# A two-layer encoder trunk on one core: arrays laid out for the kernel by the host, the opening reordered, and warm-up matmuls on TensorE

## What is computed

```
x += 0.5 * SwiGLU(RMSNorm(x))        # D_FF = 2816
x += Mixer(RMSNorm(x))               # layer 0: pooling || Hyena long convolution; layer 1: 2-D neighbourhood attention
x += 0.5 * SwiGLU(RMSNorm(x))
swiglu(x) = (silu(x @ wg) * (x @ wu)) @ wd
rmsnorm(x) = x * rsqrt(mean(x*x) + 1e-6) * g
```

## Time and profile before

| | |
|---|---|
| time, median of 3 runs | 1912.54 us (1911.01 to 1912.54) |
| span of the profiled execution, first to last instruction | 1909.3 us |
| around the span, to the median | 3.2 us |
| PE busy (matmul) | 1887.2 us, 99% |
| DVE / ACT / POOL busy | 921.8 / 647.1 / 79.7 us |
| DMA | 180.34 MB, mean 94 GB/s |
| chain that ended last | PE 98%, DVE 1% |

### The profile page before, as it was taken

How to read it: one execution, slowest core, us unless ns; L and a number is a source line. 1 busy time by engine, 2 the same in 40 slices (tenths; PEclk the granted TensorE clock), 3 DMA queues, 4 the chain that set the end, 5 groups by cost and what they waited for, 6 DMA issues and landing times.

```text
span 1909.3 us, 23383 instructions
## 1 busy us (share of the span) xinstructions
PE 1887.2 (99%) x8579; PEld 1537.3 (81%) x8579; DVE 921.8 (48%) x1166; ACT 647.1 (34%) x859; POOL 79.7 (4%) x63
## 2 busy tenths in 40 slices
PE   6999999999999999999999999999999999999999
PEld 5888888878688888888888888888777788888887
DVE  6444444366555444433544443336776654444321
ACT  4333332233243333322333232225656533333221
POOL 2000000012300000000000000001111000000000
PEclk9999999999999999999999999999999999999999
DMA  6333333243033333333233334323222133333331
GB/s 174 92 98 99 99 105 101 81 133 92 30 91 97 99 97 91 113 97 97 78 99 99 97 91 120 91 83 94 64 82 83 55 100 93 94 99 103 112 107 52
DMA packets 349165, 180.34 MB, mean 94 GB/s; under 512 B 12922, under 2 KB 347525, under 8 KB 349126
## 3 DMA queue, kind: packets, MB, share of 16 engines
q1 hardware_dynamic: 333504, 169.89, 30.6%
q10 hardware_dynamic: 15622, 9.93, 2.0%
HBM read 177.70 MB, written 3.93 MB: 95 GB/s over the span
## 4 chain that ended last, share of the span: by engine, by line
PE 98%; DVE 1%; DMA 0%; ACT 0%; issue 0%; ACTq 0%
PE bank L832 31%; PE bank L836 30%; PE bank L835 30%; PE bank L957 1%; PE bank L1138 1%; PE bank L1122 1%; PE bank L970 1%; PE bank L948 1%; DVE xl L584 0%; DMA vrow<-in_v_params 0%; PE bank L978 0%; PE bank L1110 0%; PE bank L937 0%; PE bank L885 0%; PE bank L1088 0%; PE bank L922 0%
## 5 line engine op out<-in xcount | busy, mean ns | idle before, releaser
L295 DVE TENSOR_TENSOR wl<-raw,wh 128x1024 fp32r<-128x1024 f32 (+1 forms) x296 | 393.4, 1329 | 685.5 <-ACT wh L288 684.1
L832 PE MATMUL bank<-xh,wh 128*128 128x512 f32 x1728 | 682.6, 395 | 6.7 <-DVE xl L584 6.7
L835 PE MATMUL bank<-xl,wh 128*128 128x512 f32 x1728 | 674.0, 390 | 0.0
L836 PE MATMUL bank<-xh,wl 128*128 128x512 f32 x1728 | 673.5, 390 | 0.0
L288 ACT ACTIVATE wh<-raw 128x1024 fp32r<-128x1024 f32 (+1 forms) x296 | 333.7, 1127 | 515.4 <-PE bank L836 515.0
L832 PEld LDWEIGHTS bank<-xh,wh 128*128 128x128 f32 x1728 | 324.8, 188 | 85.9 <-issue 12.9
L836 PEld LDWEIGHTS bank<-xh,wl 128*128 128x128 f32 x1728 | 325.0, 188 | 68.6
L835 PEld LDWEIGHTS bank<-xl,wh 128*128 128x128 f32 x1728 | 325.1, 188 | 66.4 <-issue 1.4
L832 PE MATMUL bank<-hh,wh 128*128 128x512 f32 x704 | 274.9, 391 | 0.0
L836 PE MATMUL bank<-hh,wl 128*128 128x512 f32 x704 | 274.0, 389 | 0.0
L835 PE MATMUL bank<-hl,wh 128*128 128x512 f32 x704 | 273.9, 389 | 0.0
(11 more groups left out here) (144 smaller groups left out, 1023.4 us busy)
## 6 DMA issues: line engine op xcount, KB each, us to landing
raw<-in_ffn_w_gate SPq DMA_DIRECT2D x88, 512.0 KB, 3.8
raw<-in_ffn_w_up SPq DMA_DIRECT2D x88, 512.0 KB, 3.9
raw<-in_ffn_w_down SPq DMA_DIRECT2D x64, 704.0 KB, 4.5
raw<-in_w_qkv SPq DMA_DIRECT2D x24, 512.0 KB, 3.8
raw<-in_w_in_ab SPq DMA_DIRECT2D x16, 512.0 KB, 3.9
raw<-in_w_out_ab SPq DMA_DIRECT2D x8, 512.0 KB, 3.6
raw<-in_w_o SPq DMA_DIRECT2D x8, 512.0 KB, 3.6
braw<-bias_by_column ACTq DMA_DIRECT2D x16, 192.0 KB, 3.8
```

What stands on the lines that cost most here:

```text
L295: dve.tensor_tensor(wl[w][:, 0:ph.kt, :], raw[r][:, 0:ph.kt, :], wh[w][:, 0:ph.kt, :].bitcast(F32), ALU.subtract).then_inc(low, 1)
L832: pe.matmul(out, wh[w][:, k, :], hi[:, at, :], start=start, stop=False)
L835: pe.matmul(out, wh[w][:, k, :], lo[:, at, :], start=False, stop=False)
L836: return pe.matmul(out, wl[w][:, k, :], hi[:, at, :], start=False, stop=stop)
```

## The change

The host lays out x (features first, 4 KB a partition and transfer), the seven weight arrays (one unit's tile is contiguous in a partition: 4 KB, or 5.5 KB for down) and the parameters (already turned). The outputs leave features first and are turned back on the host. In the kernel:

```diff
+WARM_UP = 12
-            for n in range(4):
-                sp.dma_start(xrow[:, n % 2 * 2:n % 2 * 2 + 2, half], ...).then_inc(x_in[n], 16)
+            def bring_x(n):
+                sp.dma_start(x[:, 2 * n:2 * n + 2, :].rearrange("p k t -> p (k t)"),
+                             a["x_tokens"][:, 2 * n * TOK:2 * (n + 1) * TOK]).then_inc(x_in[n], 16)
+            bring_x(0)
+            bring_weights(phases[0], 0, 0)
+            for n in range(1, 4):
+                bring_x(n)
+            for j in range(1, 4):
+                bring_weights(phases[0], 0, j)
@@ ACT
+            act.dma_start(vec[:, :], a["v_params"]).then_inc(vec_in, 16)
             act.dma_start(cst[:, :], a["c_small"]).then_inc(const_in, 16)
-            act.dma_start(vrow[:, :], a["v_params"]).then_inc(vec_in, 16)
...
-                        act.wait_ge(y_mm, d + 1)
-                        act.wait_ge(y_out[s], 32 * i + STORE_CREDIT)
-                        act.activation(ua[s][:, :], bank[2 + s][:, :], ACT.Copy).then_inc(y_copied, 1)
+                        act.wait_ge(evac, ph.group(i, j) + 1 + EVAC_CREDIT)
                         for n, y in enumerate((y_prompt, y_sample)):
+                            act.dma_start(y[:, bass.ds(d, 1), :], x[:, bass.ds(d, 1), n * SEQ:(n + 1) * SEQ])\
+                               .then_inc(y_out, 16)
...
+            act.wait_ge(vec_in, 16)
             for d in range(KD):
-                act.wait_ge(evac, d + 1 + EVAC_CREDIT)
+                act.wait_ge(x_in[d // 2], 16)
+                act.activation(xh[:, d, :], x[:, d, :], ACT.Copy, scale=col(V_NORM + d)).then_inc(xh_done, 1)
+                if d == 1:
+                    split_high(act, phases[0], 0, 0)
+            split_high(act, phases[0], 0, 1)
+            for d in range(KD):
+                if d == 4:
+                    split_high(act, phases[0], 0, 2)
                 if d >= 2:
                     act.wait_ge(acc_done, d - 1)
-                residual_parts(0, d, d % 2)
+                act.activation(sqtmp[:, d % 2, :], x[:, d, :], ACT.Square).then_inc(sq_done, 1)
+            split_high(act, phases[0], 0, 3)
+            act.wait_ge(const_in, 16)
+            norm_std(0)
+            split_high(act, phases[0], 1, 0)
+            evacuate(phases[0], 0, 0)
+            evacuate(phases[0], 0, 1)
+            split_high(act, phases[0], 1, 1)
+            evacuate(phases[0], 0, 2)
+            evacuate(phases[0], 0, 3)
             for r in range(DR):          # the seven DMAs of the bias, unchanged
...
@@ DVE
-            dve.wait_ge(vec_mm, 1)
-            dve.tensor_copy(vec[:, :], bank[7][:, 0:V_ALL]).then_inc(vec_done, 1)
+            dve.wait_ge(vec_in, 16)
...
-                dve.wait_ge(x_mm, d + 1)
-                dve.tensor_copy(x[:, d, :], bank[d][:, :]).then_inc(evac, 1)
-            split_low(dve, phases[0], 0, 0)
+                part_low(0, d)
+                if d == 1:
+                    split_low(dve, phases[0], 0, 0)
+            split_low(dve, phases[0], 0, 1)
             for d in range(KD):
-                part_low(0, d)
                 if d == 4:
-                    split_low(dve, phases[0], 0, 1)
+                    split_low(dve, phases[0], 0, 2)
+                add_squares(0, d, d % 2)
+            split_low(dve, phases[0], 0, 3)
+            norm_factor(0)
+            evacuate(phases[0], 0, 0)
+            split_low(dve, phases[0], 1, 0)
+            evacuate(phases[0], 0, 1)
+            sums_cleared(0)
+            evacuate(phases[0], 0, 2)
+            split_low(dve, phases[0], 1, 1)
+            evacuate(phases[0], 0, 3)
@@ PE
-            (transpose of vrow, 32 transposes of x, turn_y and its hooks)
+            pe.wait_ge(mean_of_done, 1)
+            for _ in range(WARM_UP):
+                pe.matmul(bank[7][:, 0:P], mean_of[:, :], mean_of[:, :], start=True, stop=True)
...
+                    if name == "up0":
+                        unit(ph, 0, 0, waits=[(xl_done, k + 1) for k in range(KD)])
+                        unit(ph, 0, 1)
+                        unit(ph, 0, 2, hooks={6: lambda: norm_mean(0)})
+                        rest = range(3, ph.per)
@@ POOL
-            for d in range(KD):
-                (sum of the squares)
```

More of the change, by code:

```diff
@@ L87, in plan @@
               Phase("w_o", 2, 4, KD, [0, 1, 2, 3]), up(3), down(3)]
-    unit, group, uses = 0, KD, [0] * 4
+    unit, group, uses = 0, 0, [0] * 4
     for n, ph in enumerate(phases):
@@ L214, in build_trunk @@
         qh_done, ql_done, kh_done, kl_done = sem("qh_done"), sem("ql_done"), sem("kh_done"), sem("kl_done")
-        mask_done, gqk_done, y_ready, y_mm, y_copied = (sem("mask_done"), sem("gqk_done"), sem("y_ready"), sem("y_mm"),
-                                                        sem("y_copied"))
-        y_out = [sem(f"y_out{s}") for s in range(2)]
+        mask_done, gqk_done, y_out = sem("mask_done"), sem("gqk_done"), sem("y_out")
         block = ctx.enter_context(nc.Block())
@@ L233, in unit_source, with bring_weights @@
             if ph.name.startswith("up"):
[L234 removed]
+                return (wu if j % 2 else wg)[ffn_of[ph.name], bass.ds(2 * i + j // 2, 1)]
             if ph.name.startswith("down"):
[L236 to L237 removed]
+                half = KF // 2 * P
+                return wd[ffn_of[ph.name], bass.ds(2 * i + j // 2, 1), :, j % 2 * half:(j % 2 + 1) * half]
             if ph.name == "w_in":
[L239 removed]
+                return w_in[bass.ds((3 - j) * KH + i, 1)]
             if ph.name == "qkv":
[L241 to L242 removed]
+                return w_qkv[bass.ds(j * KD + i, 1)]
+            return (w_out if ph.name == "w_out" else w_o)[bass.ds(4 * i + j, 1)]
         @block.sync
         def _(sp):
[L246 to L250 removed]
+            def bring_x(n):
+                sp.dma_start(x[:, 2 * n:2 * n + 2, :].rearrange("p k t -> p (k t)"),
+                             a["x_tokens"][:, 2 * n * TOK:2 * (n + 1) * TOK]).then_inc(x_in[n], 16)
+            def bring_weights(ph, i, j):
+                sp.dma_start(raw[j][:, 0:ph.kt, :].rearrange("p k c -> p (k c)"),
+                             unit_source(ph, i, j).rearrange("o p c -> (o p) c")).then_inc(raw_in[j], 16)
+            bring_x(0)
[4 more added lines that the diff above has]
+                bring_weights(phases[0], 0, j)
             def load(ph, i):
@@ L254, in load @@
                     sp.wait_ge(low, ph.unit(i, j) - 2 + LOW_CREDIT)
-                    sp.dma_start(raw[j][:, 0:ph.kt, :], unit_source(ph, i, j)).then_inc(raw_in[j], 16)
+                    bring_weights(ph, i, j)
             for ph in phases:
-                if ph.name == "w_in":
+                if ph.name == "up0":
+                    with sp.Fori(1, ph.iters) as i:
+                        load(ph, i)
+                elif ph.name == "w_in":
                     for i in range(ph.iters):
@@ L304, in phase_loop @@
         def phase_loop(eng, ph, body, after_first=None, first=0):
-            if after_first or ph.name in NORM_OF or ph.name == "w_o":
+            if ph.name == "up0":
+                first = 1
+            elif after_first or ph.name in NORM_OF or ph.name == "w_o":
                 body(0, False)
@@ L538, in _ @@
                         act.activation(ah[:, 4 + c, :], x0[:, c, :], ACT.Copy).then_inc(ah_done, 1)
-            for s in range(2):
-                act.wait_ge(y_out[s], 16 * KD + STORE_CREDIT)
+            act.wait_ge(y_out, 32 * KD)
         @block.vector
@@ L589, in residual_low, with add_squares @@
                 part_low(norm, d)
+                add_squares(norm, d, parity)
+            def add_squares(norm, d, parity):
                 dve.wait_ge(sq_done, chunk_base(norm) + d + 1)
-                dve.wait_ge(acc_done, chunk_base(norm) + d)
+                if not isinstance(d, int) or norm or d:
+                    dve.wait_ge(acc_done, chunk_base(norm) + d)
                 dve.tensor_tensor(sqacc[:, :], sqacc[:, :], sqtmp[:, parity, :], ALU.add).then_inc(acc_done, 1)
@@ L653, in evacuate @@
                     dve.wait_ge(unit_done, ph.unit(i, j) + 1 + UNIT_CREDIT)
-                    out = ga[parity][:, :] if ph.name == "down3" else x[:, bass.ds(d, 1), :]
+                    out = x[:, bass.ds(d, 1), :]
                     dve.scalar_tensor_tensor(out=out, in0=bank[b][:, :], scalar=factor, in1=x[:, bass.ds(d, 1), :],
@@ L902, in filter_layer @@
                     pe.wait_ge(filt_in, 64)
+                    pe.wait_ge(const_in, 16)
                 else:
@@ L916, in turn_u @@
                 last.then_inc(ut_mm, 1)
[L918 to L923, removed]
             def attention(p, projects, attends, last_one):
@@ L1051, in hooks_at @@
                         return {2: lambda: filter_layer(j - 1)}
[L1053 to L1056, removed]
                     return {}
                 def first(ph=ph, name=name):
-                    if name in NORM_OF:
+                    if name == "up0":
[3 more added lines that the diff above has]
```

(22 more changed lines are left out.)

45 lines of the change are left out of this document (9 added, 36 removed).

## The result

The changed kernel takes 1919.14 us (median of 5; 1918.41 to 1919.61) against 1911.04 us for the kernel before (median of 5): ratio 1.0039, 95% interval 1.0026 to 1.0052. It is slower, by 8 us, where 1900.5 (1894.5 to 1904.5) had been forecast with 0.95 on faster. The profiled span went from 1909.3 to 1916.6 us, so 7.3 us have to be found.

What follows compares the result with a forecast made beforehand. PE was taken as the bound, 99% busy, so time could be won only in the opening, the eight `turn_y` and the tail: 1912.5 - 14.75 - 3.3 - 1.35 + 5.4 + 2.0 = 1900.5 us, range 1894.5 to 1904.5.

Steps and rivals of the forecast that it cites:

- The 480-byte shift of hh and its neighbours: Tiles hh and those behind it move by 480 bytes in SBUF; costed at 0.
- The rival of the other side: Dense 4 KB weight writes hold up PE's reads; a loss from 4.7 ns per affected product, 1931 us at 12 ns; 2%.
- The row with and without a landing transfer: Middle: half a microsecond holds four matmuls with no transfer or weights landing at 344 GB/s, so the layout is worth 0.
- The opening: From the start to unit (0,1) on PE: new load order and no transposes, 14.75 us won.
- U: Moment unit (0,1) starts on PE: 30.41 us before, forecast 15.65, bounds 14.3 to 17.7.
- my lower bound: Opening loads land 1.3 us apart, the best rate seen, putting unit (0,1) at 14.3 us; 1.6 was taken.
- an idle stretch of 3.2 us: PE's gap between warm-up, ending near 6 us, and first product at 9.2; clock expected to stay at the upper level.
- low clock in unit (0,0): First unit at low clock ends near 17.4 us, 1.75 later; with slow landings some 1903.5 us in all, 15%.
- The bias DMAs: Seven issues hold ACT 8.0 us ahead of `split_high` (1,2), so PE stalls 5.4 us near 44 to 49 us.
- clock after it: After the new PE stall near 44 to 49 us the clock falls, costing 2.0 us; rival that it holds, 20%.
- The norm's chain: Mean, root, reciprocal, then `split_low` (1,0) ready at U + 16.6 us, wanted at U + 17.2: in time by 0.6.
- The ending: Seven `turn_y` gone save 3.3 us; first output DMA right after DVE's sum saves 1.35.

Runs made afterwards that it cites:

- run 1: The changed kernel plus an unused 480-byte tile behind seed, so hh, hl and all behind them stand where they stood before the change: 1903.07 us.
- run 2: The kernel before plus one unused 32-byte tile behind gqk, so hh and all behind it stand 32 bytes higher: 1928.26 us.
- run 11: The kernel of run 8 with the seven weight arrays back in the old layout of 512-byte rows: 1894.51 us.
- run 8: The kernel of run 4 with 26 warm-up matmuls in place of 12: 1892.72 us.
- Run 3: The changed kernel with the seven bias DMAs moved from ACT's queue to SP's, behind the first eight loads: 1910.64 us.
- run 4: The changed kernel with both edits, the unused 480-byte tile and the bias DMAs on SP's queue: 1896.18 us.
- run 6: The kernel of run 4 with 32 bytes between hh and hl, so hl is off by 32 bytes: 1906.33 us.
- run 9: The kernel of run 8 with 32 bytes ahead of x, so all operands of the three-fold products move together: 1894.05 us.

## Why the prediction was wrong

- **The step that failed**: "The 480-byte shift of hh and its neighbours I also cost at 0." The prediction saw the shift, put its price at nothing and gave no reason. It cost 16.4 us in the span (runs 1 and 2: 16 and 16.3), more than all of the gain. No row of before could price it, since xh's and hh's products both step fast there; then it should have had a range and a rival: at 5% of a step for 2496 products, 28 us.
- **The rival of the other side** had the right form, some ns on every product with a small threshold, and the wrong mechanism: it was the place of the tiles, not the dense writes. The row with and without a landing transfer was read rightly: run 1 has the dense writes and the fast step, and run 11 shows that the weights' layout is worth 0.
- **The opening**: U at 17.99, forecast 15.65. Landings were better than assumed: DMA ran near 400 GB/s, the 1.3 us a transfer of my lower bound and not the 2.0 of an unchanged rate. But the first product came at 10.20 and not at 9.2, since ACT began with a table load of 1.28 us (at 5.31) that the sum didn't have. The main loss was the clock: I took an idle stretch of 3.2 us as harmless because the clock had fallen only after 4.6 before; the stretch was 4.2 long, and the clock fell 2.1 us after the warm-up's end. In run 1 the same twelve matmuls ended only at 7.09, the stretch was 3.2 us, as forecast, and the clock fell all the same, at 10.7, when the first product had already begun. One fall doesn't give a safe length. My case "low clock in unit (0,0)" put U at 17.4. That run 8, where the clock held, has U at 15.75 is in part luck: faster landings made up for the table load, and PE's own 24 matmuls ended last and not the split.
- **The bias DMAs**: right in place and size. Issues 7.6 us (forecast 8.0), stall 5.8 (5.4), clock after it 1.6 (2.0). The Trainium skill (DMA: Bandwidth & Descriptors, Issuing engines are not separate DMA queues) calls issue time usually small beside the transfer. Here it was 7.6 us on ACT, and the split behind it came so late that PE waited 5.8. Run 3 took the stall away and won 8.5 us.
- **The norm's chain**, in time by 0.6 us by my sum, was late by 0.4: I had the root's table load done earlier, and it came after the mean (at 28.61 us, 1.28 long).
- **The ending**: forecast -4.65, measured -4.8.

Without the shift the change would have been at 1903.07 (run 1), 2.6 us above the forecast and within its range. The base had a flaw of its own: the sum started from 1912.5, the upper of the two values between which the kernel before changes, while its profile's span of 1909.3 goes with executions of about 1911.0. From there the same terms give 1899.0, and run 1 lies 4.1 above it; of such misses U's 2.3 in the changed kernel is the largest.

## What to carry to other kernels

Removing or adding a small tile moves everything allocated behind it, and TensorE's step can depend on it: compare the step of the same product in both traces first, and when PE's busy time rises with fewer instructions, look at addresses before queues. Keep the operand that is loaded and all those that stream at a multiple of 256 bytes from each other, with an explicit pad if need be. Before a block of DMA issues is moved on a computing engine, price the engine's sequencer time and ask which split stands behind it; and a warm-up has to last until the first product (in run 4, 12 matmuls that ended 3.3 us ahead of it were worth 0; 26 that reached it were worth 1.8 us).

## What was not expected of the hardware

- float32r products of 128 x 512 stepped some 0.227 us at one distance, modulo 256 bytes, of the loaded and the streamed operand in SBUF, and 2.3 to 6.8 ns (1 to 3%) more at the other distances tried. That distance alone doesn't account for run 6. By the tiles' sizes, rounded up to 32 bytes, the fast distance is a multiple of 256 for xh as for hh; the weight load's own duration didn't change (187 to 188 ns).
- TensorE's clock fell 4.6 us after PE's last work in the kernel before, 2.1 and 2.0 us after it in the changed one, and 3.6 us after the warm-up in run 1 (window 10 to 11, PEclk 0.85), 0.4 us into the next product.
- A short fall of the clock after the attention's waits cost 1.6 us in run 4's profile. It is absent in run 8's and there in run 9's, though both have the same opening, and executions of one kernel lie about as far apart.
